# One seven-product form moved from the first to the second down pair of an MLP, bank reads placed before a weight split, and the joins of transposed halves moved from VectorE to ScalarE

## The reference

```python
u = rms_norm(h, mlp_norm_w[layer]) @ w_up[layer]          # 256 x 2048 @ 2048 x 8192
h = h + jnp.square(jax.nn.relu(u)) @ w_down[layer]        # 256 x 8192 @ 8192 x 2048
```

## Time and profile before

| | before |
|---|---|
| median of 3 runs (lowest, highest) | 1999.79 us (1996.29, 2002.52) |
| the profiled execution | 1996.55 us |
| its span, first to last instruction | 1994.5 us |
| granted PE clock | 0.999 |
| PE / DVE / ACT busy | 99% / 75% / 60% |
| first matmul of the MLP to last matmul's end | 1295.17 to 1991.37 us |

### The profile page before, as it was taken

The page is one execution under the profiler, slowest core; times in us unless marked ns, Lnnn a source line. Parts: engine busy times, 40 slices in busy tenths (PEclk is TensorE's granted clock), DMA queues, the critical chain, the costliest instruction groups (busy, mean ns, idle before and its releaser), DMA issues.

```text
span 1994.5 us, 25717 instructions
## 1 busy us (share of the span) xinstructions
PE 1975.6 (99%) x9007; PEld 1627.6 (82%) x9007; DVE 1500.3 (75%) x1748; ACT 1199.9 (60%) x1383; POOL 175.2 (9%) x179
## 2 busy tenths in 40 slices
PE   9999999999999999999999999999999999999999
PEld 8888888888887888888888888888788788778877
DVE  5777777777888777676675665668888878888887
ACT  6666666667776555556764444657556645745663
POOL 2110120112231211110000000000000000000000
PEclk9999999999999999999999999999999999999999
DMA  7777887889987666666896667857667666766764
GB/s 248 216 196 203 213 202 203 222 232 237 247 232 215 192 199 192 197 190 190 233 241 202 200 209 234 235 180 226 209 196 228 199 203 193 220 202 193 230 202 157
DMA packets 332193, 419.52 MB, mean 210 GB/s; under 512 B 147248, under 2 KB 147696, under 8 KB 331840
## 3 DMA queue, kind: packets, MB, share of 16 engines
q1 hardware_dynamic: 331184, 415.23, 72.1%
q10 hardware_dynamic: 448, 2.24, 0.3%
q0 software_dynamic: 464, 0.77, 0.2%
HBM read 382.46 MB, written 2.16 MB: 193 GB/s over the span
## 4 chain that ended last, share of the span: by engine, by line
PE 84%; DVE 8%; DMA 3%; ACT 2%; issue 2%; SPq 1%; DVEq 0%; ACTq 0%
PE ps L796 20%; PE ps L798 20%; PE ps L797 20%; PE ps L1095 7%; PE ps L1096 7%; PE ps L1097 7%; DVE wlo L2373 2%; DVE t_lo__92 L2383 2%; DMA raw<-in_w_down 1%; DMA f_half<-r_half 1%; DMA raw<-in_w_up 1%; PE ps L975 1%; DVE wlo L2377 1%; DVE wlo L2368 1%; PE ps L744 1%
## 5 line engine op out<-in xcount | busy, mean ns | idle before, releaser
L1808 DVE TENSOR_TENSOR wlo<-raw,whi 128x1024 fp32r<-128x1024 f32 x450 | 569.6, 1272 | 328.1 <-ACT whi L1204 326.6
L1204 ACT ACTIVATE whi<-raw 128x1024 fp32r<-128x1024 f32 x450 | 473.4, 1057 | 324.2 <-PE ps L798 313.4
L796 PE MATMUL ps<-whi,xT_hi 128*128 128x512 f32 x1268 | 498.3, 393 | 0.0
L798 PE MATMUL ps<-whi,xT_lo 128*128 128x512 f32 x1268 | 493.8, 389 | 0.0
L797 PE MATMUL ps<-wlo,xT_hi 128*128 128x512 f32 x1268 | 493.5, 389 | 0.0
L1687 ACT ACTIVATE whi<-raw 128x1024 fp32r<-128x1024 f32 x187 | 193.6, 1055 | 146.9 <-PE ps L1097 146.9
L798 PEld LDWEIGHTS ps<-whi,xT_lo 128*128 128x128 f32 x1268 | 238.0, 188 | 50.0
L796 PEld LDWEIGHTS ps<-whi,xT_hi 128*128 128x128 f32 x1268 | 238.1, 188 | 48.8 <-issue 1.4
L797 PEld LDWEIGHTS ps<-wlo,xT_hi 128*128 128x128 f32 x1268 | 238.2, 188 | 47.6
L2373 DVE TENSOR_TENSOR wlo<-raw,whi 128x1024 fp32r<-128x1024 f32 x156 | 184.2, 1218 | 37.1 <-ACT whi L1687 37.0
L1095 PE MATMUL ps<-whi,fT_hi 128*128 128x512 f32 x416 | 164.3, 395 | 12.2 <-DVE fT_lo L2492 7.3
(11 more groups left out here) (358 smaller groups left out, 2883.4 us busy)
## 6 DMA issues: line engine op xcount, KB each, us to landing
raw<-in_w_in SPq DMA_DIRECT2D x319, 512.0 KB, 4.2
raw<-in_w_up SPq DMA_DIRECT2D x128, 512.0 KB, 4.3
raw<-in_w_down SPq DMA_DIRECT2D x128, 512.0 KB, 4.7
raw<-in_w_ssm_out SPq DMA_DIRECT2D x64, 512.0 KB, 4.1
raw<-in_w_attn_out SPq DMA_DIRECT2D x32, 512.0 KB, 4.1
raw<-in_w_out SPq DMA_DIRECT2D x32, 512.0 KB, 4.3
arow<-arows SPq DMA_DIRECT2D x16, 512.0 KB, 4.8
x_in<-in_x SPq DMA_DIRECT2D x4, 512.0 KB, 8.1
```

Of the source, the lines that this page charges most:

```text
L796: mm(dst, xh, whi[sl][:, kk, :], start=(s == 0 and kk == 0), stop=False)
L798: last = mm(dst, xl, whi[sl][:, kk, :], start=False, stop=(s == US - 1 and kk == UK - 1))
L1204: A(whi[s % SLOTS][:, :, :], raw[s % SLOTS][:, :, :], ACT.Copy).then_inc(hi_ready, 1)
L1808: V.tensor_tensor(wlo[s % SLOTS][:, :, :], raw[s % SLOTS][:, :, :], fp(whi[s % SLOTS][:, :, :]), ALU.subtract).then_inc(lo_ready, 1)
```

## The change

Line numbers of the code in this section are those of the two files.

It moves one seven of each group: down A has now one, at position 0, and down B three, at 0, 3 and 5, in natural order; the three forms of a down group are made and rounded at the places that `FORMS_MADE`, `FORMS_HI` and `FORMS_LO` list. `u_sums` (and `p1_copy` with it) stands at quad 5 of up B instead of 6, and at quad 6 of down B instead of 5. After an up pair the bank reads come before the first `mlp_lo` of the new pair. The two copies of `f_join` are made on ACT, at the head of `f_hi`. In a seven quad PE waits for the first part of `wlo` before p1 and for the second before p3, and DVE makes the two parts with two instructions.

```diff
-DOWN_SEVEN = (0, 3)
+DOWN_SEVEN = (0, 3, 5)
+DOWN_SEVEN_FIRST = (0,)
-DOWN_ORDER_LATE = (0, 1, 2, 4, 3, 5, 6, 7)
+DOWN_ORDER_LATE = (0, 1, 2, 3, 4, 5, 6, 7)
-    return (UP_SEVEN, UP_SEVEN_LATE, DOWN_SEVEN, DOWN_SEVEN)[m % 4]
+    return (UP_SEVEN, UP_SEVEN_LATE, DOWN_SEVEN_FIRST, DOWN_SEVEN)[m % 4]
-SUMS_AT = (6, 6, 5, 5)
+SUMS_AT = (6, 5, 5, 6)
+FORMS_MADE = ((1, 4), (2, 1), (2, 3))
+FORMS_HI = ((1, 4), (2, 2), (2, 4))
+FORMS_LO = ((1, 5), (2, 5), (2, 6))
...
                     def p1():
+                        pe.wait_ge(hi_ready, n + 1)
+                        pe.wait_ge(lo_ready, n + 1)
...
                         product(0, *x_tile(1, 0), *w_tile(2))
+                        pe.wait_ge(hi_ready, n + 2)
+                        pe.wait_ge(lo_ready, n + 2)
                         product(1, *x_form(3), *w_tile(3)).then_inc(unit_used, 1)
...
             def f_hi(m, a):
-                act.wait_ge(f_joined, 2 * p + a + 1)
+                n = 2 * p + a
+                act.wait_ge(r_turned, 32 * n + 32)
+                if n:
+                    act.wait_ge(fT_lo_done, n)
+                    act.wait_ge(sums_made, forms_before(n))
+                src = f_half1 if a else f_half0
+                for pl in range(2):
+                    i = A(halves(f_st[:, :, :].rearrange("p c t -> p (c t)"))[:, pl, :].rearrange("p (c t l) -> p c t l", c=4, t=NTOK),
+                          src[:, pl, :, :].rearrange("p (t c) l -> p c t l", t=NTOK), ACT.Copy)
+                i.then_inc(f_joined, 1)
+                act.wait_ge(f_joined, n + 1)
                 A(fT_hi[:, 4 * k:4 * k + 4, :], f_st[:, :, :], ACT.Copy).then_inc(fT_hi_done, 1)
...
-                dve.wait_ge(hi_ready, n + 2)
-                V.tensor_tensor(lo[:, 1:4, :], src[:, 1:4, :], fp(hi[:, 1:4, :]), ALU.subtract).then_inc(lo_ready, 2)
+                for i, part in enumerate((slice(1, 3), slice(3, 4))):
+                    dve.wait_ge(hi_ready, n + i + 1)
+                    V.tensor_tensor(lo[:, part, :], src[:, part, :], fp(hi[:, part, :]), ALU.subtract).then_inc(lo_ready, 1)
...
                     if m and j == 0:
-                        mlp_lo(*nxt, only=0)
+                        if (m - 1) % 4 >= 2:
+                            mlp_lo(*nxt, only=0)
                         bank_sums(m - 1)
+                        if (m - 1) % 4 < 2:
+                            mlp_lo(*nxt, only=0)
                         mlp_lo(*nxt, only=1)
```

More of the change, by code:

```diff
@@ L99, with forms_before @@
 H_SUMS = 1 if UP_SEVEN else 0
-SUMS_AT = (6, 6, 5, 5)
+SUMS_AT = (6, 5, 5, 6)
+FORMS_MADE = ((1, 4), (2, 1), (2, 3))
+FORMS_HI = ((1, 4), (2, 2), (2, 4))
+FORMS_LO = ((1, 5), (2, 5), (2, 6))
 JOIN_AT = {1: (3, 5), 2: (3, 4)}
 LOW_AT = {1: (4, 6), 2: (3, 4)}
+def forms_before(n):
+    return 4 * H_SUMS + sum(3 for q in range(PAIRS // 4) for s in DOWN_SEVEN if 4 * q + s // 2 < n)
 def follow(m, j, n):
@@ L1161, in p4 @@
                         product(6, *x_tile(1, 1), *t_tile(3)).then_inc(t_used, 1)
-                    pe.wait_ge(hi_ready, n + 2)
-                    pe.wait_ge(lo_ready, n + 2)
                     p1()
@@ L1786, in _ @@
                             f_hi(before, JOIN_AT[m % 4].index(j))
-                    if DOWN_SEVEN and (m % 4, j) in ((1, 4), (2, 1)):
-                        f_sums_hi(m // 4, m % 4 - 1)
+                    if (m % 4, j) in FORMS_HI:
+                        f_sums_hi(m // 4, FORMS_HI.index((m % 4, j)))
                     if m == 0 and j == 1:
@@ L2456, in h_last @@
                 V.tensor_tensor(v, v, ps[7][:, T:2 * T], ALU.add).then_inc(h_final, 1)
[L2458 to L2468, removed]
             def f_sums(q, i):
@@ L2531, in _ @@
                     nxt = follow(m, j, 1)
[L2532 to L2537, removed]
                     if early(*follow(m, j, 2)):
@@ L2547, in _ @@
                         mlp_lo(*nxt)
[L2548 to L2551, removed]
+                    if (k, j) in FORMS_MADE:
+                        f_sums(m // 4, FORMS_MADE.index((k, j)))
+                    if (k, j) in FORMS_LO:
+                        f_sums_lo(m // 4, FORMS_LO.index((k, j)))
                     if m and k in LOW_AT and j in LOW_AT[k]:
@@ L2557, in _ @@
                         u_sums(m)
-                        if m == PAIRS - 1:
-                            h_from_sums(m)
+                    if j == 7 and m == PAIRS - 1 and seven(m):
+                        h_from_sums(m)
                     if m == 0 and j == 1:
```

## The result

| | before | after |
|---|---|---|
| median (lowest, highest, runs) | 1998.94 us (1996.29, 2002.52, 4) | 1985.89 us (1985.47, 1986.15, 4) |
| profiled execution | 1996.55 | 1985.47 |
| its span | 1994.5 | 1983.4 |
| first matmul of the MLP to the end of the last one | 1295.17 to 1991.37: 696.2 | 1295.61 to 1979.20: 683.6 |
| from there to the end of the span | 3.1 | 4.2 |

The predicted time was 1986, from 1980 to 1993.

A forecast was written before the change was run, and what follows sets the result against it. PE bounds the kernel, with at most 18.6 us of waits to win. Terms 5.2 + 3.3 + 6.8 + 1.0 - 1.3 - 1.8 - 1.0 = 12.2 won gave 1984.3 or 1987.6; middle 1986, range 1980 to 1993.

The forecast's parts named there:

- What bounds it: PE, busy 99%, with equal matmuls; only its standing time in the MLP can be won, at most 18.6 us.
- The signs: Expected in the profile: `fT_lo` waits under 0.5 us each, ACT's copies near 1 us, no seven of down B waiting.
- Seven away from quad 3: Quad 3 of down A: PE's wait for a seven's late `wlo` goes, 3.3 us won.
- split of the `wlo`: p2 of down B: `wlo` in two parts makes `c_free` 0.5 earlier, 1.0 us won.
- `u_sums` behind in down B: p2 of up A: the bank read comes later, 0.66 instead of 0.24 three times, 1.3 us lost.
- Bank reads ahead: p2 of up B and down A: PE's waits for the C banks go, 5.2 us won.
- The turn, with the joins on ACT: Quad 4 of down A: the `fT_lo` wait falls from 2.1 to 0.4 us each, 6.8 won.
- `u_sums` ahead of `t_sums` in up B: Last quad of up B: a new PE wait of 0.45 us, 4 times, 1.8 lost.
- The end of down A: Quad 7 of down A: its split may come late, taken as 0.25 us 4 times, 1.0 lost.
- slow copies: Rival: ACT's join copies take 1.9 us each, only 4.6 won, about 1993; chance 0.12.
- arrears of DVE: Rival: DVE late at quad 7 and in up A, 6.0 us won, about 1992; chance 0.12.
- the join that holds ACT's queue: Rival: the second join waits for transposes with quads 6 and 7's splits behind it, over 2003 us; chance 0.04.

The follow-up runs named there:

- e3: Changed kernel with the half split of quad 1 ahead of the bank reads after up pairs too: 1991.75 us, ratio 0.9958, MLP 688.4.
- e5: Changed kernel with a seven's `wlo` made in one piece and released once: 1986.95 us, ratio 0.9938, MLP 684.7.
- e1: Kernel before with only the sevens moved (forms and sums tables to match): 1998.76 us beside 2000.44, ratio 0.9986, MLP 691.6.
- e12: Changed kernel with sevens, their order and two forms as before, all else as changed: 1992.63 us, ratio 0.9968, MLP 692.2.
- e2: Changed kernel with the joins back on DVE, ahead of the next quad's split: 1990.06 us, ratio 0.9947, MLP 686.3.
- e4: Changed kernel with `u_sums` and `p1_copy` of up B back at quad 6, behind quad 7's split: 1986.95 us, ratio 0.9925, MLP 684.3.
- e13: Changed kernel with other access patterns of the joins on ACT, values wrong, one execution: copies 1352 ns writing every other element, 1045 ns dense.

## Why the prediction was right, and where its steps were off

- *What bounds it* held. The matmuls are equal in number, and the gain is PE's standing time. The list of waits gave the most that there was to win, 18.6, and I had priced each wait with its 0.27 that the rows hide; the differences of the matmuls' starts give 18.9. The signs came but for two: a wait on `fT_lo` is 0.59 to 0.88, not under 0.5, and ACT's copies take 1.29 to 1.35, not 1. No seven of down B waits.
- *Seven away from quad 3*, *split of the `wlo`*, *`u_sums` behind in down B*: each within 0.1 of the forecast. *Bank reads ahead*: 5.6 where 5.2 were forecast, since a seventh wait, 0.37 at p2 of the first down A, was not in my list. e3 brings back 3.2 of these 5.6, and e5 the 1.0 of down B. As places in the sum they were right, as separate causes not: the wait at quad 3 goes with the move alone (e1) and with the rest alone (e12), and the two are worth less apart than together. The forecast was of the whole, and did not need the split; had I been asked for one part I would have been wrong, as my expectations for e1, e2 and e12 were.
- *The turn, with the joins on ACT* was mis-sized: 4.6 won, not 6.8. The chain was right: in the second group ReLU begins 1.75 after T (forecast 1.8), the first `r_half` ends at 9.7 (9.8), and ACT starts the join right behind the second half of quad 4's split, at 1569.90 or 16.9 after T (16.9). The landing is less far ahead of that than I had it, T + 16.4: in the third group, where T is 1723.30, the join waits for it until 17.1 after T (its line stands with e4), and the wait on `fT_lo` is 0.88 instead of 0.59. The term at fault is the copy at 0.95: it takes 1.29 in a row, 1.35 alone, for its writes (e13). Twice 0.34 on 0.4 gives 1.1 a group; 0.9 was measured. The joins put 41 us on ACT, not 30.
- The rule of the Trainium skill ("ScalarE: Activation LUTs", section "Rules for kernel authors"), which gives the simple operations to VectorE, would, read for a copy, have had the joins left there. The copies are indeed faster there, 0.75 beside 1.35 us; but e2 shows that this kernel loses 2.7 by it, since the queue behind the join counts for more than the copy.
- *`u_sums` ahead of `t_sums` in up B*: 0.4 to 0.8 each, 0.6 in the mean, where 0.45 was forecast. *The end of down A*: I had 1.0, there is none. Quad 4's larger wait gives DVE 0.5 more time there, and the second transposes landed before ACT asked for them (0.2 of idle time before a join in the whole MLP), so my chain of median landings was too late.
- *Left out*: the tail, 1.1 lost, and the half clock, 1.6 won in the profiled execution. The waits gave 10.6 where I had 12.2, 1.6 too much; the half clock happens to make that up. The profiled execution was to come to 1984.3 and came to 1985.47.
- *Luck*: the predicted 1986 is the middle between 1984.3, counted from the profiled execution, and 1987.6, counted from the median; nothing in the sum says that the middle is right. That it stands 0.1 from the measured 1985.89 is chance, for single terms were off by up to 2.2.
- The rivals: slow copies came true by a third of their price, arrears of DVE to 0.15 a group, and the join that holds ACT's queue not at all. The two rivals said to win "5 to 6" win 4.6 and 6.0 by their own sums, and the chances named for a faster kernel add up to 0.84, not 0.8.

## What to carry to other kernels

Waits of one engine that stand in a row in a program are not a list of savings: one that waits for a chain with its own start takes back what was saved ahead of it, so follow the chain to the last wait before counting the first, and remove the parts that lie in front of the same wait together. When a copy waits for a DMA, what matters of the engine it is put on is what stands behind it in that queue, more than how fast the engine copies. And a matmul that waits costs more than the row says: the overlap hides part of it, and in this kernel one near 2 us was in some executions followed by 3.4 us at half the clock.

## What the runs showed of the hardware that I had not expected

The half clock came behind waits of PE of 1.82 us (before), 2.2 (e4) and 2.5 to 2.6 (e12, two of four), began at once (e4) or up to 1.4 us after PE had resumed (e12), lasted 3.4 us each time and cost 1.6. It did not come behind each long wait: not behind the other two of 2.5 to 2.6 in e12, not behind the other three of 1.8 before, and not behind six of 1.7 to 1.9 in e1, e2, e3 and e13. What decides it, these profiles do not show. It goes with how differently the times of the kernels scatter. e1, with four waits of up to 1.8 us, has in its 10 runs a mean granted clock of 1.0 in those of 1994.62, 1995.46 and 1995.56 us, 0.998 or 0.999 in those of 1998.3 to 1999.6, and 0.996 in that of 2004.15. My estimate from these figures: a mean of 0.998 over 1997 us is 4 us of clock missing and 0.996 is 8, and such runs are 3 to 5 and 9 us longer than the three at 1.0. The changed kernel, with none over 0.9, has 4 runs within 0.7 us. So part of the 13 us between the medians is this, and the profiled executions, 11.1 apart, hold less of it.

ACT writes every other 16-bit element at 1.35 us a 1024-column copy, and densely at 1.045, while reading every other one shows no such cost: `r_half` takes 1.89 for 2048 columns, which is twice the dense 1045 less 0.2.
